# One run of jobs from the hybrid mixer's output to the cross-attention's queries, and norms without joins, in a two-block transformer on one core

## What is computed

```python
def second_block(x, mem, ...):
    for l in range(2):
        h = rmsnorm(x, norm_mix_w[l])
        x = x + hybrid_mixer(h, w_in[l], ...)          # ends with cat @ w_out
        h = rmsnorm(x, norm_xattn_w[l])
        mem_n = rmsnorm(mem, norm_mem_w[l])
        x = x + memory_cross_attention(h, mem_n, w_q[l], w_kv[l], w_o[l])
        h = rmsnorm(x, norm_ffn_w[l])
        if l == 0:
            x = x + swiglu(h, ffn_w_gate[0], ffn_w_up[0], ffn_w_down[0])
        else:
            x = x + moe_swiglu(h, router_w[0], moe_w_gate[0], moe_w_up[0], moe_w_down[0])
    return rmsnorm(x, norm_final_w)

def rmsnorm(x, w):
    return x * rsqrt(mean(x * x, axis=-1) + 1e-6) * w
```

## Time and profile before

| | us |
|---|---|
| median of 3 runs | 2579.53 |
| lowest, highest | 2578.74, 2583.67 |
| profiled execution | 2579.66 |
| its span in the trace | 2577.9 |

### The profile page before, as it was taken

How to read it: one execution, slowest core, us unless ns; L and a number is a source line. 1 busy time by engine, 2 the same in 40 slices (tenths; PEclk the granted TensorE clock), 3 DMA queues, 4 the chain that set the end, 5 groups by cost and what they waited for, 6 DMA issues and landing times.

```text
span 2577.9 us, 43172 instructions
## 1 busy us (share of the span) xinstructions
PE 2277.6 (88%) x16284; PEld 2118.2 (82%) x16284; DVE 1788.4 (69%) x2088; ACT 1373.8 (53%) x1571; POOL 68.7 (3%) x116
## 2 busy tenths in 40 slices
PE   7769999878699996868799796969999999999997
PEld 6569999766599996857799794859898898898996
DVE  5477775645766765774566586457888888888886
ACT  4345664344455553454333335336676677676765
POOL 0000000100000002000000100000000000000000
PEclk9889999999899998989999897989999999999999
DMA  7329998521299996414355641518999999999993
GB/s 268 107 105 379 372 375 314 151 82 59 103 354 359 373 336 155 160 48 155 98 181 172 157 158 46 176 36 289 311 333 363 336 369 327 336 368 329 340 365 117
DMA packets 335558, 609.68 MB, mean 237 GB/s; under 512 B 11024, under 2 KB 266848, under 8 KB 310736
## 3 DMA queue, kind: packets, MB, share of 16 engines
q1 hardware_dynamic: 329696, 590.84, 65.9%
q0 software_dynamic: 5056, 13.23, 2.3%
q10 hardware_dynamic: 560, 2.10, 0.2%
HBM read 605.08 MB, written 1.05 MB: 235 GB/s over the span
## 4 chain that ended last, share of the span: by engine, by line
PE 78%; DVE 11%; ACT 5%; issue 3%; DVEq 2%; POOLq 0%; DMA 0%; ACTq 0%; POOL 0%
PE psum L129 16%; PE psum L131 16%; PE psum L130 16%; PE psum L1999 9%; PE psum L2035 9%; PE psum L2023 2%; DVE weight_ring_rounded L116 1%; PE psum L497 1%; DVE h_cf L2873 1%; ACT scores L804 1%; PE psum L2351 1%; PE psum L756 1%; PE psum L2544 1%; PE psum L1706 1%; PE psum L319 1%
## 5 line engine op out<-in xcount | busy, mean ns | idle before, releaser
L1759 DVE TENSOR_TENSOR weight_ring_rounded<-weight_ring,weights_high_rounded 128x2048 fp32r<-128x2048 f32 x264 | 604.3, 2292 | 91.5 <-ACT weights_high_rounded L1754 91.5
L1754 ACT ACTIVATE weights_high_rounded<-weight_ring 128x2048 fp32r<-128x2048 f32 x264 | 505.1, 1916 | 100.9 <-PE psum L131 97.7
L129 PE MATMUL psum<-weights_high_rounded,scores_rounded 128*128 128x256 f32 x1408 | 408.2, 290 | 5.0 <-issue 3.9
L131 PE MATMUL psum<-weights_high_rounded,scores_rounded 128*128 128x256 f32 x1408 | 401.0, 285 | 0.0
L130 PE MATMUL psum<-weight_ring_rounded,scores_rounded 128*128 128x256 f32 x1408 | 400.7, 285 | 0.0
L2096 DVE TENSOR_TENSOR weight_ring_rounded<-weight_ring,weights_high_rounded 128x2048 fp32r<-128x2048 f32 x128 | 292.9, 2292 | 96.8 <-ACT weights_high_rounded L2091 96.8
L129 PEld LDWEIGHTS psum<-weights_high_rounded,scores_rounded 128*128 128x128 f32 x1408 | 272.4, 193 | 9.8 <-issue 5.3
L130 PEld LDWEIGHTS psum<-weight_ring_rounded,scores_rounded 128*128 128x128 f32 x1408 | 272.5, 194 | 3.4
L131 PEld LDWEIGHTS psum<-weights_high_rounded,scores_rounded 128*128 128x128 f32 x1408 | 272.5, 194 | 0.0
L1999 PE MATMUL psum<-weights_high_rounded,scores_rounded 128*128 128x256 f32 x1024 | 262.6, 294 | 4.2 <-issue 1.9
L131 PE MATMUL psum<-weights_high_rounded,xT_rounded 128*128 128x512 f32 (+3 forms) x688 | 260.9, 379 | 0.0
(11 more groups left out here) (539 smaller groups left out, 4025.0 us busy)
## 6 DMA issues: line engine op xcount, KB each, us to landing
weight_ring<-in_moe_w_gate_dram SPq DMA_DIRECT2D x152, 1024.0 KB, 7.0
weight_ring<-in_moe_w_up_dram SPq DMA_DIRECT2D x152, 1024.0 KB, 9.0
weight_ring<-in_moe_w_down_dram SPq DMA_DIRECT2D x152, 1024.0 KB, 8.9
weight_ring<-in_w_in_dram SPq DMA_DIRECT2D x20, 1024.0 KB, 6.3
weight_ring<-in_ffn_w_gate_dram SPq DMA_DIRECT2D x11, 1024.0 KB, 5.3
weight_ring<-in_ffn_w_up_dram SPq DMA_DIRECT2D x11, 1024.0 KB, 5.4
weight_ring<-in_ffn_w_down_dram SPq DMA_DIRECT2D x11, 1024.0 KB, 4.9
weight_ring<-in_w_out_dram SPq DMA_DIRECT2D x8, 1024.0 KB, 5.1
```

The costliest lines, as they stand in the source:

```text
L129: nc.tensor.matmul(out, lh, rh, start=start, stop=False)
L131: return nc.tensor.matmul(out, ll, rh, start=False, stop=stop)
L1754: self.c.nc.scalar.activation(ring.high(self.s0 + q, 1, SLOT), ring.view(self.p0 + q, 1, SLOT), ACT.Copy).then_inc(ring.high_ready, 1)
L1759: self.c.nc.vector.tensor_tensor(ring.low(self.p0 + q, 1, SLOT), ring.view(self.p0 + q, 1, SLOT), ring.high(self.s0 + q, 1, SLOT).bitcast( ...
```

## The change

Four things:

1. `cross_attention` has one list of jobs from the output projection to the queries: output half 0, turning of the memory's columns, output half 1, norm of x, keys, turning of the x columns, values, queries. Two joins go, steps of TensorE are new in `projection`, and the weights are claimed in the new order.
2. The norm behind the cross-attention is made in halves of columns: the squares and gain products of half 0 stand between the two jobs of the last projection, those of half 1 behind it. In layer 0 the turning of the columns is in the same list; `dense_ffn` has no norm and join of its own, and TensorE waits for all columns. In layer 1 `flat_moe` has no `rms_scales` of its own. The last projection has no join.
3. `pre_norm` writes the unused squares to SBUF instead of PSUM, uses banks 4 to 7, takes a root of a constant first, and has no join behind it; the first job of the hybrid projection waits for the columns in halves.
4. In `SplitExpert.vector` the next window comes behind the copy of the rows.

```diff
+def half_norm_steps(c, h, gain, landed, ready):
...
+    def squares(act):
+        act.wait_ge(*ready())
+        for t in range(TT):
+            nc.scalar.activation(junk[:, t, half], c.x[:, t, half], ACT.Square, accum_out=c.stats[:, h, t, 0:1])
+        act.drain().then_inc(*summed.up())
+        if h == 0:
+            nc.scalar.activation(c.var[:, 3, 0, :], c.ones[:, 0:1], ACT.Sqrt)
+
+    def scale(dve):
+        dve.wait_ge(*landed)
+        dve.drain()
+        nc.vector.tensor_tensor(c.scaled[:, :, half], c.x[:, :, half], gain[:, half].unsqueeze(1).broadcast_to([P, TT, 512]), ALU.mult)
+        if h == 1:
+            dve.wait_ge(*summed.at(2))
+            c.dve(nc.vector.tensor_tensor(var, sums[0], sums[1], ALU.add))
+            nc.vector.tensor_scalar(var, var, 1.0 / D, RMS_EPS, ALU.mult, ALU.add).then_inc(*rooted.up())
...
+    first = [Step("act", squares), Step("dve", scale)]
+    return first if h == 0 else first + [Step("act", root), Step("dve", invert)]
...
+def column_steps(c, j, y, dst, banks, first):
...
+    def turn(pe):
+        pe.wait_ge(*c.sig(f"rms_diagonal_{j}").at(1))
+        for (k, t), bank in zip(groups, banks):
+            for i in range(4):
+                last = nc.tensor.matmul(c.psum[:, bank, i * P:(i + 1) * P], y[:, t, (k + i) * P:(k + i + 1) * P],
+                                        c.diag[:, j, t, :], start=True, stop=True)
+            last.then_inc(*turned.up())
...
+class RowsByHalves(Rows):
...
+        for i, tile in enumerate(self.tiles):
+            pe.wait_ge(*columns.at(TT * (i + 1)))
+            self.one_tile(c, pe, pair, i, tile)
...
         self.order(lambda q: self.low(dve, q, i), combine, part,
                    lambda q: next_window and self.low(dve, q, i + 1))
-        if next_window:
-            next_window()
         self.used(dve, self.p0 + self.down(self.chunks - 1), i)
         nc.vector.tensor_copy(self.rows[:, 512:], c.psum[:, 5, :]).then_inc(self.rows_dve.sem, 1)
         if next_window:
+            next_window()
             self.low(dve, self.up(0), i + 1)
...
 def pre_norm(c, gain):
 
-    rms_scales(c, 0, c.x, gain, c.scaled, c.sig("gain_landed").now())
-    rms_columns(c, [(0, c.scaled, c.xs)], join=False)
+    junk = c.S[:, 1, :, :].rearrange("p k t -> p (k t)").rearrange("p (t d) -> p t d", t=TT)
+    nc, blocks = c.nc, {"pe": c.block.tensor, "act": c.block.scalar, "dve": c.block.vector}
+
+    @c.block.scalar
+    def _(act):
+        nc.scalar.activation(c.var[:, 3, 0, :], c.ones[:, 0:1], ACT.Sqrt)
+    for step in rms_steps(c, c.x, gain, c.scaled, c.sig("gain_landed").now(), lambda: c.sig("gain_landed").now(), junk) + \
+            column_steps(c, 0, c.scaled, c.xs, (4, 5, 6, 7), 0):
+        blocks[step.who](step.run)
...
-        Rows(c.xs, w, Z_V + HV, HV + 2 * ML_H, "dve", take_edge(vo[:, :, HV:], 0, 2 * ML_H)),
+        RowsByHalves(c.xs, w, Z_V + HV, HV + 2 * ML_H, "dve", take_edge(vo[:, :, HV:], 0, 2 * ML_H)),
...
-    c.join(pool=False)
...
         rms_scales(c, 1, mem, c.gain[:, :], rows, c.sig("mem_landed").now())
-        projection(c, before, then=lambda: claim(c, jobs))
-        rms_scales(c, 0, c.x, c.bias[:, :], c.scaled, c.sig("gain_landed").now())
-        rms_columns(c, [(1, rows, memT), (0, c.scaled, c.xs)])
-
+        junk = c.S[:, 1, :, :].rearrange("p k t -> p (k t)").rearrange("p (t d) -> p t d", t=TT)
+        projection(c, before[:1] + column_steps(c, 1, rows, memT, (4, 5, 6, 7), 0) + before[1:] + rms_steps(
+            c, c.x, c.bias[:, :], c.scaled, c.sig("gain_landed").now(), lambda: c.sig("results_taken_dve").at(2), junk) + [
+            Step("pe", lambda pe: pe.wait_ge(*columns.at(TT * 2)))] + keys + column_steps(c, 0, c.scaled, c.xs, (5, 7, 2, 3), TT * 2) + values + [
+            Step("pe", lambda pe: pe.wait_ge(*columns.at(TT * 4)))] + queries)
...
-        projection(c, jobs)
...
-        projection(c, jobs, then=after)
+        landed, taken = c.sig("gain_landed").now(), c.sig("results_taken_dve")
+        steps = [half_norm_steps(c, h, c.bias[:, :], landed, lambda h=h: taken.at(h + 1)) for h in range(2)]
+        columns = column_steps(c, 0, c.scaled, c.xs, (4, 5, 6, 7), 0) if after else []
+        projection(c, jobs[:1] + steps[0] + jobs[1:] + steps[1] + columns, join=False, then=after)
...
 def dense_ffn(c, start):
...
-        pre_norm(c, c.bias[:, :])
-        c.join()
...
-        rms_scales(c, 0, c.x, c.bias[:, :], c.scaled, c.sig("gain_landed").now())
```

More of the change, by code:

```diff
@@ new lines, in column_steps, with copies, run @@
+def column_steps(c, j, y, dst, banks, first):
+    nc = c.nc
+    turned, high, done = c.sig("rms_turned"), c.sig("rms_high"), c.sig("rms_split")
+    groups = [(k, t) for k in (0, 4) for t in range(TT)]
+    def turn(pe):
[5 more added lines that the diff above has]
+            last.then_inc(*turned.up())
+    def copies(name):
+        def run(eng):
+            for g, (k, t) in enumerate(groups):
+                split_copy(c, name, eng, tuple(d[:, k:k + 4, t * P:(t + 1) * P] for d in dst),
+                           c.psum[:, banks[g], :].rearrange("p (k t) -> p k t", k=4), turned.at(first + g + 1), high, done)
+        return run
+    return [Step("pe", turn), Step("act", copies("act")), Step("dve", copies("dve"))]
@@ L546, in multiply, with one_tile @@
         for i, tile in enumerate(self.tiles):
[L547 to L559, removed]
+            self.one_tile(c, pe, pair, i, tile)
+    def one_tile(self, c, pe, pair, i, tile):
+        tile.wait(pe)
+        for t in range(TT):
+            ts = slice(t * P, (t + 1) * P)
+            out = c.psum[:, 2 * pair + t, 0:self.width]
+            for k in range(self.per):
+                g = i * self.per + k
+                start, stop = g == 0, g == self.kt - 1
+                if self.split:
+                    last = three_products(c.nc, out, [x[:, g, ts] for x in self.xT],
+                                          (tile.high[:, k, :], tile.low[:, k, :]), start, stop)
+                else:
+                    last = c.nc.tensor.matmul(out, self.xT[:, g, ts], tile.whole[:, k, :], start=start, stop=stop)
+        last.then_inc(c.ring.used, 1)
     def out(self, c, pair):
@@ L574, in multiply @@
         super().multiply(c, pe, pair)
+class RowsByHalves(Rows):
+    def multiply(self, c, pe, pair):
+        columns = c.sig("rms_split")
+        assert self.per == KD // 2
+        for i, tile in enumerate(self.tiles):
+            pe.wait_ge(*columns.at(TT * (i + 1)))
+            self.one_tile(c, pe, pair, i, tile)
 class Cols(Job):
@@ L680, in _ @@
     def _(pe):
-        for j, job in enumerate(jobs):
+        for job in order:
+            if isinstance(job, Step):
+                if job.who == "pe":
+                    job.run(pe)
+                continue
+            j = jobs.index(job)
             if j >= 4:
@@ L1478, in two_products @@
             pe.wait_ge(hidden_ready.sem, hidden_ready.base + (j - 1) + U * i)
+        if j == 0:
+            pe.wait_ge(*columns.at(2 * TT))
         for tile, bank in ((gate_tile(j), 0), (up_tile(j), 2)):
```

48 lines of the change are left out of this document (45 added, 3 removed).

## The result

The changed kernel takes 2556.4 us (median of four, 2554.3 to 2559.9), the kernel before beside it 2579.6. The ratio is 0.9908, with a 95% interval of 0.9893 to 0.9924: 23.2 us less, where 26.15 were forecast. The profiled execution has a span of 2558.1 us (before 2577.9).

A forecast was written before the change was run, and what follows sets the result against it. The prediction took TensorE to bound the kernel (78% of the chain that ended last). Its terms, -8.85 - 1.5 - 1.3 + 0.7 - 1.85 - 7.35 - 6.0, summed to -26.15 us, giving 2553.4 us, range 2547 to 2564.

The forecast's parts named there:

- Stage to query products: Output projection to cross-attention, both layers: joins removed and TensorE's gaps closed, -4.45 and -4.4 us, together -8.85.
- rival 2: Merged stage starves: a key, value or query tile is split too late, 8.85 us lost, 2562.3 us; chance 0.07.
- Hybrid projections: Start of the hybrid projections, both layers: join goes, first products need half the columns, -1.5 and -1.3 us.
- Norm ahead of the dense layer: Norm by halves between last projection and dense layer, layer 0: slower by 0.7 us.
- The trap: Ahead of the dense layer: ScalarE's weight split queues behind half 0's norm, so residual half 1 starts 2.8 us late.
- Ahead of the large experts: Norm by halves between last projection and large experts, no later tile waiting: -1.85 us.
- Order in the large experts: Seven expert boundaries: VectorE copies rows before subtracting the next window, first product 1.05 us sooner each, -7.35 us.
- The clock there: Expert boundaries: all four falls of TensorE's clock to 0.50 go, 1.5 us each, -6.0 us, bounds 0 and -6.
- Rival 1: Falls of the clock at the expert boundaries stay: 2559.4 us; chance 0.12.
- Rivals 3 and 4: Large experts: weight stream holds them, 2566.8 us, chance 0.05; or VectorE becomes the bound inside each, 2620 us, chance 0.02.

The follow-up runs named there:

- the second time: The changed kernel run once more, unchanged, for a second profiled execution: 2555.4 us, ratio 0.9892 to the kernel before.

## Why the prediction was right, and where it was off

The time fell inside the range, 3.0 us above the forecast, and each step could be found in the trace. That the stretches of the table sum to -26.4, as if the forecast had been off by 0.3 us, is luck in part: the length of the cold starts added to one term what others lacked. In the order of the sum:

- **Stage to query products, -4.45 and -4.4.** Right in its mechanism: after, no product has an idle note from 1147.89 to the last query product, and the values' splits are in time, so rival 2 didn't come. The term was mis-sized. The profiles showed -6.2 and -4.6, of which 4.7 to 5.0 are the edit's and the rest is the length of the cold start. The working took the gaps from windows laid inside them; by the idle notes the three inner ones are 1.56, 0.53 and 1.66, so 3.75 us in place of 3.5, and the last goes from 1.35 to 1.03. That explains 4.1; the 0.6 to 0.9 beside it, products' own durations at the gaps, it had at 0.6.
- **Hybrid projections, -1.5 and -1.3.** Measured 0.9 and 1.2 less. The start was right or better (2.0 us ahead at the middle wait for the 1.66 of the sum, and the 0.2 to 0.45 us charged for a later diagonal didn't come: TensorE's idle note ahead of the turnings is 16.32 and 10.52 before, 16.31 and 10.53 after). The step that failed was to take the gain as still there at the stage's end, without looking at the clock behind a wait of 4.9 us inside.
- **Norm ahead of the dense layer, +0.7.** The trap came as described: split L112 at 1244.0, which is 1245.05 by the clock of the kernel before, whose projection starts 1.05 us later (forecast 1245.2), and the residual add 2.7 us late (2.8). The term was mis-sized: by TensorE's waits it costs 0.25 us. The table load took 1.28 us with the next instruction at 1243.89, 0.01 behind, so the drain that the Trainium skill, "ScalarE: Activation LUTs" (What ACT_TABLE_LOAD costs), adds to it was not seen here either.
- **Ahead of the large experts, -1.85.** The wait fell by 1.98. The stretch fell by 1.05 or 2.0, as its cold start went: 18.8 to 18.9 us in six profiles, 17.9 to 18.0 in four.
- **Order in the large experts, -7.35.** Measured -7.0: the waits fell by 1.00, not 1.05. The new releaser is the window, as its 0.1 us of margin in the forecast let one expect.
- **The clock there, -6.0.** Right that all four falls go, and the run with filling products shows the cause. The term was mis-sized by about 1 us: four falls at 1.49 us each are 6.0, but the experts won 12.0 in all, 5.0 beside the waits, and filling the gap alone won 4.9. In the changed kernel 0.44 us of the difference is a wait for a split at 1845.27, since VectorE has no slack there now; the rest I can't place. Rival 1 is out. Rivals 3 and 4 are too, but for that wait: four of the six periods behind the first are 98.9 or 99.0 us, the others 99.4 and 99.7.

The terms of the whole came to -26.15, the traces from the first turning on to -25.6 and -25.4. With the edit's own part for each term (about -9.8, -2.1, +0.25, -2.0, -7.0, -5.0) the sum is about -25.6 as well. The medians say -23.2, and -27.4 the second time; both differences from the traces are within the spread of the first thousand us, which the change hardly touches.

## What to carry to other kernels

When an instruction list is reordered, look for a wait of TensorE that ends last on a copy queued behind work that nobody needs yet; three such places in this kernel gave 12, 9 and 3 us without one instruction less. A wait is worth more than its length when the clock falls behind it: price both, and test it by filling the wait with products that don't count. Compare idle notes and stretches, not spans, since the nearly unchanged first thousand us moved by up to 11.5 us from one profile to another. A stretch wants its cold start taken off, and several profiles.

## What the runs showed of the hardware

Between the experts, 3.0 us with only eight transposes in them brought the clock down behind four of seven boundaries, in the same pattern in two programs (first, third, fifth, seventh). The gap made longer brought it down behind four as well (first, third, fifth, sixth). 2.0 us brought none in ten profiles of nine programs. Ten products of 256 columns in the gap brought none either. At a wait of 4.9 us the clock fell in all 24 stages that have one. Where it fell 4.4 to 5.2 us into the wait, 1.5 to 1.7 us of products were lost behind it; where it fell 2.0 to 4.2 us into it, 2.0 to 3.1. No run here says what sets that moment. The cold start of the same stage in the same kernel lost 1.4 us in one execution and 3.1 in the next.
